# Normed rows of M1, M2 and M3 transposed by DMA into the activation buffer, with the norm weights multiplied there

## What is computed

```python
hn = rms_norm(x, norm1_g)                      # y = x * rsqrt(mean(x*x) + eps) * g
g_b, g_c, x_a, x_l, g_l = split(hn @ w_in)     # 5 x 512 columns
out_a = g_b * causal_conv3(g_c * x_a)
out_b = rg_lru(causal_conv4(x_l) + b) * gelu(g_l)   # gated linear recurrence over time
x = x + concat([out_a, out_b]) @ w_out
x = x + square(relu(rms_norm(x, norm2_g) @ w_up)) @ w_down    # hidden width 4096
y = rms_norm(x, norm_f_g)
```

## Time and profile before

| | |
|---|---|
| median of 3 runs | 950.35 us (947.94 to 950.88) |
| the profiled execution | 944.28 us |
| its span on the slowest core (core 7) | 942.3 us |
| spans of the cores | 934.9 to 942.3 us |
| busy: PE, VectorE, ScalarE, POOL | 840.7, 485.1, 452.4, 171.1 us |
| mean granted TensorE clock | 0.952 to 0.966 |

### The profile page before, as it was taken

The page is one execution under the profiler, slowest core; times in us unless marked ns, Lnnn a source line. Parts: engine busy times, 40 slices in busy tenths (PEclk is TensorE's granted clock), DMA queues, the critical chain, the costliest instruction groups (busy, mean ns, idle before and its releaser), DMA issues.

```text
span 942.3 us, 14350 instructions; the slowest of 8 cores (934.9 to 942.3 us)
## 1 busy us (share of the span) xinstructions
PE 840.7 (89%) x4136; PEld 401.4 (43%) x4136; DVE 485.1 (51%) x846; ACT 452.4 (48%) x816; POOL 171.1 (18%) x280
## 2 busy tenths in 40 slices
PE   2777674797589999999999899999999999999997
PEld 1344332343344555544444444444444444444443
DVE  2788898899675744021024478460536756041022
ACT  3698878899548643310024566420555742053111
POOL 5022410211401432400004211000321110032100
PEclk9888887899699999999999999999999999999999
DMA  8999999999864342332449745515874507485532
GB/s 213 241 190 185 111 172 193 175 120 162 139 99 144 112 115 76 107 107 75 145 127 327 210 135 150 154 56 146 253 225 136 152 7 201 146 241 152 155 101 90
DMA packets 69196, 142.38 MB, mean 151 GB/s; under 512 B 8064, under 2 KB 8192, under 8 KB 68096
## 3 DMA queue, kind: packets, MB, share of 16 engines
q1 hardware_dynamic: 49824, 90.26, 33.4%
q0 software_dynamic: 14832, 31.73, 23.6%
q10 hardware_dynamic: 4464, 19.48, 6.4%
HBM read 151.08 MB, written 31.52 MB: 194 GB/s over the span
## 4 chain that ended last, share of the span: by engine, by line
PE 72%; DMA 7%; issue 7%; DVE 6%; ACT 6%; ACTq 1%; DVEq 0%; SPq 0%
PE ps L1057 22%; PE ps L1007 21%; PE ps L741 9%; PE ps L959 6%; PE ps L737 5%; ACT sb_t_rig L503 3%; DMA sb_ring<-wscr 2%; DMA sb_xsl<-xl 2%; PE ps L1049 2%; PE ps L682 2%; DMA sb_xsl<-xp 2%; DVE sb_t_xc L514 2%; PE ps L819 1%; PE ps L659 1%; PE ps L1067 1%
## 5 line engine op out<-in xcount | busy, mean ns | idle before, releaser
L503 ACT ACTIVATE sb_junk<-sb_xsl 128x1024 bf16<-128x1024 f32 (+1 forms) x54 | 53.4, 990 | 254.8 <-DVE sb_xsl L506 232.3
L1007 PE MATMUL ps<-sb_hT,sb_ring 128*128 128x512 bf16 (+1 forms) x896 | 173.9, 352 | 0.7 <-DMA sb_ring<-wscr 0.5
L506 POOL TENSOR_TENSOR sb_uT<-sb_rl 128x512 bf16<-128x512 bf16 x64 | 71.3, 1115 | 399.2 <-ACT sb_stat L503 220.7
L503 ACT ACTIVATE sb_rl<-ps 128x512 bf16<-128x512 f32 (+1 forms) x160 | 85.0, 551 | 121.6 <-PE ps L1007 105.4
L506 DVE TENSOR_TENSOR sb_xsl<-ps,sb_xsl 128x512 f32<-128x512 f32 (+1 forms) x50 | 40.6, 837 | 177.3 <-PE ps L1057 112.9
L1057 PE MATMUL ps<-sb_ring,sb_uT 128*128 128x512 bf16 x520 | 123.8, 379 | 0.0
L1007 PEld LDWEIGHTS ps<-sb_hT,sb_ring 128*128 128x128 bf16 x896 | 88.2, 99 | 82.3 <-issue 1.9
L1007 PE MATMUL ps<-sb_hT,sb_uS 128*128 128x512 bf16 x384 | 86.7, 384 | 0.0
L514 DVE SCALAR_TENSOR_TENSOR sb_t_xc<-sb_t_xb,sb_par,sb_t_xc 128x512 f32<-128x512 f32 (+1 forms) x108 | 77.9, 731 | 9.6 <-ACT sb_t_xc L503 8.9
L506 DVE TENSOR_TENSOR sb_uT<-sb_rl 128x512 bf16<-128x512 bf16 x64 | 27.8, 435 | 96.5 <-ACT sb_rl L503 94.1
L1057 PE MATMUL ps<-sb_uS,sb_uT 128*128 128x512 bf16 x344 | 76.9, 379 | 0.0
(11 more groups left out here) (114 smaller groups left out, 1050.4 us busy)
## 6 DMA issues: line engine op xcount, KB each, us to landing
sb_ring<-wscr SPq DMA_DIRECT2D x196, 256.0 KB, 2.6
sb_uS<-wscr SPq DMA_DIRECT2D x120, 256.0 KB, 2.7
wscr<-wall POOLq DMA_DIRECT2D x64, 256.0 KB, 25.1
sb_xsl<-xl ACTq DMA_DIRECT2D x8, 1024.0 KB, 11.1
sb_xsl<-xp ACTq DMA_DIRECT2D x16, 512.0 KB, 11.7
yp<-sb_xsl POOLq DMA_DIRECT2D x10, 512.0 KB, 8.6
sb_uT<-wall POOLq DMA_DIRECT2D x16, 256.0 KB, 41.7
wscr<-sb_uT SPq DMA_DIRECT2D x16, 256.0 KB, 30.4
```

Source lines behind the costliest of these rows:

```text
L503: return OP("act", dur, lambda e: e.activation(out=out, in_=in_, func=func, **kw), rd_, wr_)
L506: return OP(eng, dur, lambda e: e.tensor_tensor(out=out, in0=in0, in1=in1, op=op), rd_, wr_)
L1007: return lambda slot: [lambda e, kc=kc: e.matmul(out=bank_ap(b, q.N), lhsT=slot[:, kc * 128:(kc + 1) * 128], rhs=h_ap(q, True, kc, 0, q.N) ...
```

## The change

For M1, M2 and M3, in both norms, the eight transposes on PE and the VectorE instruction out of PSUM are replaced by one DMA on ScalarE's queue for each row block. It reads `hb` and writes the 128 token columns of `hT` transposed. A new strand `g_gain`, one for each tile and norm, first claims the `hT` buffer by a memset of one column on POOL, which orders the DMAs behind the last readers of the buffer; when all four DMAs are given out, it multiplies the buffer in place by the norm weight, in eight VectorE instructions of 128x512, one for each block of 128 channels, and marks the four tokens. `hb` is given back once the DMA has read it. The DMAs have a pool of four semaphores of their own. The planner books one at 0.26 MB on ScalarE's queue, and each multiply at 0.25 us. L tiles, S and M0 stay as they are.

```diff
--- before.py
+++ after.py
@@ -375,7 +375,7 @@
 
     with ExitStack() as es:
         S = Sched(nc, es)
-        for name, n in (("ring", 16), ("x", 8), ("cv", 24), ("wb", 8), ("par", 6), ("st", 8), ("stx", 8), ("sto", 2)):
+        for name, n in (("ring", 16), ("x", 8), ("tr", 4), ("cv", 24), ("wb", 8), ("par", 6), ("st", 8), ("stx", 8), ("sto", 2)):
             S.dma_pool(name, n)
         W = Weaver(S)
 
@@ -389,6 +389,7 @@
         wout_b = [Buf("wout%d" % i) for i in range(4)]
         xsl = sb("xsl", [128, 8 * D])
         xsl_b = [Buf("xs%d" % i) for i in range(14)]
+        tr_b = [[Buf("tr") for _ in range(4)] for _ in range(4)]
         hb = sb("hb", [128, 2 * D], BF16)
         hb_b = [Buf("hb%d" % i) for i in range(2)]
         NHT = 3
@@ -654,16 +655,33 @@
             W.put(P_stat, [ks])
             if t is Ms[1] and j > 1 and not second:
                 W.put(P_x, [k])
+            hT3 = hTs[hs][:, 2048 if second and t is Ss else 0:][:, 0:8 * t.hw].rearrange("p (k t) -> p k t", k=8)
+            if t in Ms[1:]:
+                yield tok(("claim", t.name, second))
+                yield DMA("act", hT3[:, :, j * 128:(j + 1) * 128], hb_ap, [hb_b[kh]], [tr_b[hs][j]], "tr", 0.26, transpose=True)
+                W.put(P_hb, [kh])
+                W.mark(("tr", t.name, second))
+                return
             (b,) = yield get(P_bank)
             pb = bank_ap(b).bitcast(BF16)
             yield PE(0.55, [lambda e, kc=kc: e.transpose(out=pb[:, kc * 128:(kc + 1) * 128], in_=hb_ap[:, kc * 128:(kc + 1) * 128],
                                                          identity=identb[:]) for kc in range(8)], [hb_b[kh], ident_b], [bank_b[b]])
             W.put(P_hb, [kh])
-            hT3 = hTs[hs][:, 2048 if second and t is Ss else 0:][:, 0:8 * t.hw].rearrange("p (k t) -> p k t", k=8)
             yield TT("dve", 1.22, hT3[:, :, j * 128:(j + 1) * 128], pb.rearrange("p (k t) -> p k t", k=8),
                      gt[:, :, None].to_broadcast([128, 8, 128]), ALU.mult, [bank_b[b], par_b], [hT_b[hs]])
             W.put(P_bank, [b])
             W.mark(done)
+
+        def g_gain(t, second):
+            hs, gt = (t.h2, g2t) if second else (t.h1, g1t)
+            yield MSET("pool", hTs[hs][:, 0:1], 0.0, [hT_b[hs]] + tr_b[hs])
+            W.mark(("claim", t.name, second))
+            yield tok(("tr", t.name, second), 4)
+            for kc in range(8):
+                o = hTs[hs][:, kc * 512:(kc + 1) * 512]
+                yield TS("dve", 0.25, o, o, gt[:, kc:kc + 1], None, ALU.mult, None, tr_b[hs] + [par_b], [hT_b[hs]])
+            for _ in range(4):
+                W.mark(("h2" if second else "h1") + t.name)
 
         def g_normL(t):
             (t.rs,) = yield get(P_rs)
@@ -700,6 +718,8 @@
                     t.h1 = NHT
                 else:
                     (t.h1,) = yield get(P_hT)
+                if t in Ms[1:]:
+                    W.spawn(g_gain(t, False), t.prio)
                 if t.lean:
                     W.spawn(g_normL(t), t.prio)
                 for n, j in enumerate(() if t.lean else (0, 2, 3, 1) if t is Ms[1] else range(t.J)):
@@ -712,6 +732,8 @@
                         t.h2 = t.h1
                     else:
                         (t.h2,) = yield get(P_hT)
+                        if t in Ms[1:]:
+                            W.spawn(g_gain(t, True), t.prio)
                     W.mark("h2got" + t.name)
                 if t is Ms[1]:
                     (t.pair,) = yield get(P_hT)
```

## The result

The changed kernel has a median of 982.54 us where the kernel before, run beside it, has 950.29 us; the ratio is 1.0334 (1.0319 to 1.035). The forecast was 941 us, in a range up to 966. The profiled execution took 981.29 us with a span of 979.4 us. By this median the kernel before has 941.2 to 941.6 us on five chips and the changed one 976.3, 34.8 us more than 941.5; by the medians of the slowest core the loss is 32 us. First the page: the engines' busy times, the slices of PE and its clock.

A forecast was written before the change was run, and what follows sets the result against it. PE was taken as the bound from 264 us on, ScalarE and VectorE before. Terms -8.9 (transposes) - 2.4 (wait) + 2.4 (before 264 us) = -8.9 us gave 941 us against 950.35, range 934 to 966.

The forecast's parts named there:

- Transposes off PE, -8.9 us: From 264 us on, 20 groups of eight transposes leave PE at 0.445 us each: 8.9 us less.
- The wait for hb, -2.4: PE's wait for normed rows, nearly all before 520.60 us: half of 4.9 us gained, bounds 0 and 4.9.
- In the chain stage ... 3 x 1.5 = 4.5 us, at full price: Before 264 us, three of M1's four transposes stand among M0's sigmoid work, costing 4.5 us; with VectorE's 2.1 back, 2.4 lost.
- h: How long one transpose holds ScalarE; taken as 1.5 us, bounds 0.33 (plain copy's issue) and 10.9 (x row's landing).
- rival (a): ScalarE held in M0's sigmoid chain, 200 to 250 us; price 3h, deciding from h = 4.5; 960 us; chance 0.20.
- the planner's new order: Sign of being wrong: the order of work the planner makes anew opens waits no earlier row shows; no size given.
- it is covered there too: At M1's first norm, later activations cost nothing, since PE has M0's output matmuls to do until 264 us.
- The step on queued instructions: Relus and sigmoid work queue behind ScalarE's transposes, POOL's squares behind the memset; both waits cost nothing from 264 us on.
- "covered" by 19.5 us: Late rows of M2's and M3's first and second norms cost nothing: 19.5 us between M3's last transposed row and up matmuls.
- Rival (b): Transposes land slowly in series, 10.5 us each, so M2's and M3's up matmuls start late; +27 us, 977 us; chance 0.13.
- a landing between 2.6 and 7.1 us: Time for a transpose to land: from 2.6 us (256 KB ring chunk) to 7.1 us (512 KB by ScalarE's queue).
- The loss of 31 us with h = 10.9: Worst bound before 264 us: 31 us lost if each transpose holds ScalarE for an x row's landing, 10.9 us.

## Why the prediction was wrong, step by step

- **Transposes off PE, -8.9 us: right in size, where it counts.** The twelve of the second norms gave 5.5 to 6.0 for 5.3.
- **The wait for hb, -2.4: not gained.** It lay in M2's first norm. That stretch, 45.07 busy us of 50 on PE before, is now the one from 550 to 600, with 34.27: other waits took its place.
- **The step that failed: "In the chain stage ... 3 x 1.5 = 4.5 us, at full price".** The term is h, sized as one number for each transpose alone. 1.26 us is what a quiet queue asks, near the 1.5 taken; but the second transpose, behind the first and an x row that had not landed, was held 12.1 to 15.5 us on the eight cores. Three holds of 2.06, 15.49 and 1.26 on the slowest core are 18.8 us for the 4.5 of the sum. This is rival (a), given 0.20, in its place, and past its point of 3 x 4.5 = 13.5; not by its mechanism of one h for all, since two of the three were near 1.5. The price of the first two rows by themselves was 13.1 us. Of some 16 us by which they make M0's last mix late on core 3, about 12 are the hold; the other 4 come without it, perhaps from the planner's new order, which the prediction named as a sign of being wrong and gave no price.
- **Second, "it is covered there too", of M1's late rows.** PE's cover was looked at (M0's output matmuls), and it was there; VectorE's was not. Its multiplies wait in order for a landing of 24.8 us, not 2.6 to 7.1, with M0's additions to x behind them: 15.95 us. The step on queued instructions had named ScalarE's and POOL's queues only. The price of the last two rows by themselves was 11.3 us.
- **Third, first norms of M2 "covered" by 19.5 us.** The cover was that of a second norm, between last row and up matmuls. M2's first norm has none in this order: 3.7 us became 10.1, behind a last row that itself came 5.4 us late. The price was 11.5 us beside the second norms; in the changed kernel, from M1's projection to M2's up matmuls, 6.1 net of what the transposes give there. M3's first norm had similar landings (11 to 14 us) and lost only its own gain. Rival (b), with slow transfers in series, would have put it in the second norms; they landed in 4.2 us (median) in the kernel that has them alone, and cost nothing. Its 10.5 us for each (the prediction's text calls it the third rival, it is the second) was not seen in any second norm of the changed kernel, where the longest on the slowest core was 5.3.
- **The multiply at 0.35 us** was right (0.353), and a landing between 2.6 and 7.1 us held for the median from 300 us on (5.0) and for 15 of the 20, not for the five of 10.9 to 15.4.
- **Bounds.** The loss of 31 us with h = 10.9 was in the text, as a bound that the range then left out, on the ground that a plain copy is issued in 0.33 us. That row told nothing of a transposing DMA.
- **Left open:** 0.9 us of the 34.8, which is within what a sum over separate kernels can tell; what makes M0's mix 4 to 6 us late without a hold; all of the 24 us that leaving out every multiply gave back (M1's alone 7, M2's alone 5); and whether the second norms alone beat the kernel before on the slowest core. By the spans they do, by 5.5 to 6 us; but five of six executions took 961 to 963 us, against 946 and 948 in two of the eleven of the kernel before on that chip and 968 to 970 in the other nine, so by the metric the gain is not shown.

## What to carry to other kernels

Before moving work to a DMA, ask of each engine that issues it or reads its result what stands behind it in order, and how loaded the DMA engines are there: a landing time read from a quiet stretch is not that of a busy one, and here a transpose paid for whatever stood unfinished ahead of it on its queue. Move such work only where its reader has slack in the order as it is (here the second norms), and leave it where the chain of a recurrence passes through the issuing engine. A median over a queue's holds or landings hides the one that costs.

## What the runs showed of the hardware

A transposing DMA of 128x1024 bf16 from SBUF to SBUF held its issuer for 1.23 to 1.34 us on a quiet queue (12 of 12 in the kernel with second norms alone, slowest core) and landed 4.2 us after its issue (median; 3.1 at best, 9.1 at worst); a plain load was issued in 0.33. Beside conversions of f32 weights by POOL's queue six of eight, in M1's first norm and in M3's second with the added conversions, landed after 12.6 to 26.3 us; without conversions, at a DMA share of 1.03 to 1.05, five of eight took 10.9 to 15.4. The next one on the queue, some 3 to 7 us behind, was held up to 15.5 us beside conversions and 3.9 to 5.4 us in M2's first norm (eight cores of the changed kernel). With 24 of them q10 has some 25,000 packets more (29,808; 4,464 before), about 1,056 for each transpose of 256 KB. The Trainium skill, Advanced Engine Details and Errata, section "X-Bar Transpose (TRN2)", calls such transfers as fast as ordinary ones; here a ring chunk of the same 256 KB landed in 2.8 us and a transpose in 4.2 to 5.0 (medians), so the trace does not agree. In place, a multiply by a value per partition of 128x512 took 0.353 us in bf16 (median of 48, at most 1.13), against 0.48 in f32.
